# Chunk rounds of a hybrid mixer: queries turned and squared by ScalarE, solved blocks stored twice, row minima in nine visits

## The chip, the cores and the metric

One core of a Trainium2 chip runs the whole kernel in one launch. The metric is the device time of an execution in microseconds (us), and the median over several runs counts. Engines are named as in the profile: PE (TensorE matmuls), PEld (its weight loads), DVE (VectorE), ACT (ScalarE), POOL (GpSimd) and SP (SyncE, which issues the DMAs here). Each engine works through its own list in order and waits on semaphores.

## The reference

One layer on x (1024 tokens, width 1024), all in float32:

```
h    = rms_norm(x);  proj = h @ w_in
gdn  : q,k,v = silu(causal_conv(proj)); l2-normalised q,k; 4 heads of 128
       per chunk: A = strictly lower (beta k k^T * decay)
                  w = solve(I + A, beta k exp(g)); u = solve(I + A, beta v)
       v_new = u - w S;  o = (q exp(g)) S + (q k^T * decay) v_new;  S = S exp(g_last) + k_dec^T v_new
       o = rms_norm(o) * silu(gate)
pool : trailing-window means minus the token, a 64x64 map per group
mla  : 4 heads, q,k of 96, v of 64; softmax over all keys of chunks up to the query's own
x    = x + concat(gdn, pool, mla) @ w_out
x    = x + (silu(h2 @ w_gate) * (h2 @ w_up)) @ w_down,   h2 = rms_norm(x)
```

## The kernel before

The kernel runs in stages. The input projection makes tiles of 128 columns for all tokens. The chunk rounds do the delta rule and the attention together. The output projection and the feed-forward network follow, where PE works on matmuls of 512 columns almost without a pause.

**The rounds.** A chunk has 128 tokens here (eight chunks, i = 0 to 3 and b = 0 or 1, chunk 2i + b), all four heads at once. Chunk b has two PSUM banks, `U[b]` and `W[b]`. The stages of one chunk, by their names in the orders: `pre` (ACT squares q, from `qkvf` into `kd`), `qk` (PE: k times q into W; then the sums of q's squares by eight one-column instructions, L2322, into U), `turn` (PE transposes k and v), `m0` (PE turns the solved diagonal blocks `N0` by multiplying with the identity, L2334; ACT copies them to `M0`, a view of `M_`, L1379), `x1`, `y1`, `m1`, `x2`, `y2` (the inverse is put together from blocks: products on PE, copies on ACT, differences on DVE), `ks` (k and q times the state S), `tr` (the inverse applied), `av` (attention in the chunk and the new state), `oms`, `on` and `ot` (norm and turn of the output). The 32x32 diagonal blocks of all chunks are solved beforehand by DVE (`base_inverses`, 31 steps, L1804 and L1807), written to DRAM (`inverse_kept`, L783) and read back chunk by chunk as `N0` (L811 and L795).

**The attention.** For a head, the score products `st:g.kt` (L2393) go to banks 5 and 6, ACT takes the exponential (L1402), and `pv:g.kt` (L2405) multiplies by the values into bank 7. The exponential needs a bound for each query: the minimum of negated scores. `mx:t.part` (L2237) computes the scores of query tile t with the queries along the partitions into bank 4, and DVE reduces them (L1787). Twelve such visits make a head. `mr` then multiplies the minima, broadcast along one side, with the identity (L2245, two visits of four matmuls), so that they stand as a row, and ACT copies the row into row 96 of the queries (`low_row`, L1327). Head i + 1 has its maxima in round i; head 0 has them between the matmuls of the last projections (`FIRST_MAXIMA`), on banks 4 and 5 in turn.

**The order.** `PE_ORDER`, `ACT_ORDER`, `DVE_ORDER` and `POOL_ORDER` are written out by hand, stage by stage, as `stage:which:round`. SP goes through `PE_ORDER` too and issues a chunk's next loads at `ks`, `tr` and `av`, and the loads of a head at `st:0.3`. After the orders the stages of the last chunk (`AFTER_ROUNDS`) are spread over the output projection's first matmuls (L2432).

Of the kernel before, what the change touches and what calls it, by code (L numbers as in the profile page):

```python
# [13 lines left out]
P = 128  # L14
# [47 lines left out]
def hybrid_block(nc, logs_d, e_d, a_d, diag_d, n_d, qkv_d, q_d, k_d, mask_d, x2_d, hid_d, hs_d, wt_d, x, positions, attn_norm, w_in, conv_w, a_log, dt_bias, gdn_out_norm, pool_w, pool_scale,  # L62
# [27 lines left out]
    ident_r = Region(c.at).take("ident_r", [P, P], f32r)  # L90
# [17 lines left out]
    q_low = c.take("q_low", [P, TT], f32r)  # L108
# [59 lines left out]
    n_base = r.take("n_base", [P, BASE, BASE])  # L168
    solve_tmp = Region(R3_REST + 8 * 1024).take("solve_tmp", [P, BASE * BASE // 4])
# [74 lines left out]
    assert r.at <= R1 + 104 * KB  # L244
    A_, B_ = [A0, A1], [B0, Region(R1 + 110 * KB).take("B1", [P, 4, P])]
# [36 lines left out]
    with ctx:  # L282
# [83 lines left out]
        logs_kept, kk_done = sem("log_sums_kept"), sem("kk_done")  # L366
# [20 lines left out]

        def maxima(h):
            tiles = [("mx", (t, part), h) for g in GROUPS for t in range(4 * g + 3, 4 * g - 1, -1) for part in range(g + 1)]
            return tiles + [("mr", g, h) for g in GROUPS]  # L390

        LOW_TILES = [w for st, w, _ in maxima(0) if st == "mx"]

        def low_bank(w, h):
            return 4 if h else 4 + LOW_TILES.index(w) % 2

        UNITS = [(g, kt) for g in GROUPS for kt in range(4 * g + 4)]
        mp = Steps(sem("att_max_pe"), [f"mx{w[0]}.{w[1]}" if st == "mx" else f"mr{w}" for st, w, _ in maxima(0)])
        md = Steps(sem("att_max_dve"), [n for g in GROUPS for n in
                                        [f"low{t}.{part}" for t in range(4 * g + 3, 4 * g - 1, -1) for part in range(g + 1)] +  # L400
                                        (["lows"] if g else [])])
        ma = Steps(sem("att_max_act"), [f"row{g}" for g in GROUPS])
# [15 lines left out]
        def entries(text):  # L418
# [8 lines left out]
            st:1.0:0 st:1.1:0 mx:7.0:1 pv:1.0:0 mx:7.1:1 pv:1.1:0 st:1.2:0 mx:6.0:1 st:1.3:0 st:1.4:0 st:1.5:0  # L427
            mx:6.1:1 pv:1.2:0 mx:5.0:1 st:1.6:0 pv:1.3:0 mx:5.1:1 pv:1.4:0 mx:4.0:1 qk:0:0 qk:1:0 st:1.7:0 turn:0:0
            turn:1:0 st:0.0:0 pv:1.5:0 mx:4.1:1 pv:1.6:0 m0:0:0 m0:1:0 x1:0:0 mx:3.0:1 st:0.1:0 x1:1:0 mx:2.0:1
            pv:1.7:0 st:0.2:0 st:0.3:0 mx:1.0:1 y1:0:0 pv:0.0:0 pv:0.1:0 mx:0.0:1 m1:0:0 mr:1:1 x2:0:0 y1:1:0 mr:0:1  # L430
            y2:0:0 st:1.0:1 ks:0:0 pv:0.2:0 mx:7.0:2 m1:1:0 tr:0:0 x2:1:0 pv:0.3:0 mx:7.1:2 av:0:0 mx:6.0:2 pv:1.0:1
            y2:1:0 st:1.1:1 st:1.2:1 mx:6.1:2 ks:1:0 st:1.3:1 mx:5.0:2 st:1.4:1 st:1.5:1 ot:0:0 mx:5.1:2 tr:1:0
            qk:0:1 mx:4.0:2 turn:0:1 av:1:0 mx:4.1:2 m0:0:1 pv:1.1:1 pv:1.2:1 x1:0:1 pv:1.3:1 y1:0:1 mx:3.0:2
            pv:1.4:1 st:1.6:1 m1:0:1 st:1.7:1 pv:1.5:1 x2:0:1 ot:1:0 st:0.0:1 y2:0:1 qk:1:1 ks:0:1 turn:1:1 st:0.1:1
            tr:0:1 mx:2.0:2 m0:1:1 st:0.2:1 pv:1.6:1 st:0.3:1 mx:1.0:2 x1:1:1 pv:1.7:1 mx:0.0:2 av:0:1 y1:1:1
            pv:0.0:1 mr:1:2 pv:0.1:1 pv:0.2:1 m1:1:1 pv:0.3:1 st:1.0:2 x2:1:1 mr:0:2 st:1.1:2 y2:1:1 mx:7.0:3 ot:0:1
# [201 lines left out]
        def _(sp):  # L638
# [87 lines left out]
            for m in range(1, IN_ALL + KEEP_LAG):  # L726
# [1844 lines left out]
```

## Time and profile before

| | |
|---|---|
| median of 3 runs | 1221.44 us (1221.03 to 1224.62) |
| profiled execution | 1224.1 us, span 1222.3 us |
| PE busy | 1203.0 us, 98% |
| DVE, ACT, POOL busy | 809.7, 447.0, 397.6 us |
| chunk rounds | 307.9 to about 476.5 us of the span |

A row of the timeline gives the start, the time from the first instruction's start to the last one's end, the engine, the line and the number of merged instructions. Matmuls overlap, so the time that one takes from PE is read from one start to the next. A float32 matmul is two instructions, a transpose one. "Idle before" with a releaser in brackets is a wait.

### The profile page before, as it was taken

How to read it: one execution, taken by the hardware profiler on the slowest of the kernel's cores; microseconds unless marked ns; L12 is line 12 of the kernel's file. 1: busy time of each engine (PE TensorE's matmuls, PEld its weight loads, DVE VectorE, ACT ScalarE, POOL GpSimd, SP SyncE). 2: the span in 40 equal slices, each digit the busy share in tenths (PEclk: the TensorE clock that was granted, in tenths of full speed). 3: DMA queues.
4: the chain of work that ended last, by engine and by line, in shares of the span. 5: the costliest groups of instructions: out<-in, count | busy, mean ns of one | idle time of the engine just before them, and what ended most of it. 6: DMA issues, size and time to landing. Idle time of an engine off the chain costs nothing.

```text
span 1222.3 us, 16782 instructions
## 1 busy us (share of the span) xinstructions
PE 1203.0 (98%) x6225; PEld 989.2 (81%) x6225; DVE 809.7 (66%) x1235; ACT 447.0 (37%) x730; POOL 397.6 (33%) x363
## 2 busy tenths in 40 slices
PE   8999999999999999999999999999999999999998
PEld 7887777887788888888788888888888887888877
DVE  6537777898567764445756656565565688777686
ACT  6322322442334232244533333333333353435242
POOL 6001111540112221015736656675565446000000
PEclk9999999999999999999999999999999999999999
DMA  8311344672842310324147465644674369565544
GB/s 251 96 36 35 104 128 123 194 230 79 259 121 75 92 53 1 121 103 128 46 138 232 164 207 181 215 171 139 223 289 151 100 211 308 165 199 168 173 127 169
DMA packets 191779, 183.54 MB, mean 150 GB/s; under 512 B 19853, under 2 KB 148227, under 8 KB 191698
## 3 DMA queue, kind: packets, MB, share of 16 engines
q1 hardware_dynamic: 191574, 182.43, 47.2%
q8 instruction: 50, 0.82, 0.3%
q14 instruction: 31, 0.25, 0.1%
q10 hardware_dynamic: 124, 0.04, 0.0%
HBM read 125.70 MB, written 55.68 MB: 148 GB/s over the span
## 4 chain that ended last, share of the span: by engine, by line
PE 90%; DVE 5%; ACT 1%; issue 1%; POOL 1%; DMA 1%; DVEq 0%; POOLq 0%; ACTq 0%
PE ps L2522 33%; PE ps L2126 18%; PE ps L2527 14%; PE ps L2432 5%; PE ps L2295 3%; PE ps L2393 3%; PE ps L2405 3%; PE ps L2102 1%; DVE wop_lo L1989 1%; DVE xop L1973 1%; PE ps L2300 1%; PE ps L2237 1%; PE ps L2197 1%; PE ps L2093 1%; DMA wd_raw<-in_w_down 1%
## 5 line engine op out<-in xcount | busy, mean ns | idle before, releaser
L2522 PE MATMUL ps<-xop,wop_hi 128*128 128x512 f32 x1232 | 381.4, 391 | 1.7 <-DVE wop_lo L1989 1.0
L2522 PEld LDWEIGHTS ps<-xop,wop_hi 128*128 128x128 f32 x1232 | 230.7, 188 | 52.8 <-DVE wop_lo L1989 2.3
L2522 PE MATMUL ps<-xop,wop_lo 128*128 128x512 f32 x616 | 240.4, 390 | 0.0
L2527 PE MATMUL ps<-dop,wop_hi 128*128 128x512 f32 x440 | 136.9, 392 | 3.6 <-DVE x L2071 3.4
L2522 PEld LDWEIGHTS ps<-xop,wop_lo 128*128 128x128 f32 x616 | 115.6, 188 | 24.9
L1989 DVE TENSOR_TENSOR wop_lo<-w_sumS,wop_hi 128x512 fp32r<-128x512 f32 (+1 forms) x104 | 85.7, 827 | 69.2 <-ACT wop_hi L1462 69.2
L1989 DVE TENSOR_TENSOR wop_lo<-w_pair,wop_hi 128x512 fp32r<-128x512 f32 (+1 forms) x76 | 86.1, 1134 | 37.2 <-ACT wop_hi L1462 37.2
L2126 PE MATMUL ps<-act_hi,w_hi 128*128 128x512 f32 x320 | 104.0, 406 | 0.0
L2071 DVE TENSOR_TENSOR x<-x,ps 128x512 f32<-128x512 f32 x112 | 76.6, 684 | 39.2 <-PE ps L2527 39.0
L2527 PEld LDWEIGHTS ps<-dop,wop_hi 128*128 128x128 f32 x440 | 81.9, 188 | 24.2 <-DVE wop_lo L1989 4.2
L2126 PE MATMUL ps<-act_lo,w_hi 128*128 128x512 f32 x320 | 98.7, 390 | 0.0
L2126 PE MATMUL ps<-act_hi,w_lo 128*128 128x512 f32 x320 | 98.6, 389 | 0.0
L2527 PE MATMUL ps<-dop,wop_lo 128*128 128x512 f32 x220 | 86.0, 391 | 0.0
L1462 ACT ACTIVATE wop_hi<-w_sumS 128x512 fp32r<-128x512 f32 (+1 forms) x104 | 63.2, 609 | 58.5 <-PE ps L2522 42.8
L2126 PEld LDWEIGHTS ps<-act_hi,w_hi 128*128 128x128 f32 x320 | 58.7, 188 | 14.7 <-issue 2.6
L2126 PEld LDWEIGHTS ps<-act_lo,w_hi 128*128 128x128 f32 x320 | 60.1, 188 | 12.8
L2126 PEld LDWEIGHTS ps<-act_hi,w_lo 128*128 128x128 f32 x320 | 60.1, 188 | 12.7
L1462 ACT ACTIVATE wop_hi<-w_pair 128x512 fp32r<-128x512 f32 (+1 forms) x76 | 46.4, 611 | 60.2 <-PE ps L2522 47.8
L1582 DVE TENSOR_TENSOR w_lo<-raw,w_hi 128x1024 fp32r<-128x1024 f32 x20 | 25.6, 1281 | 53.2 <-ACT w_hi L1263 53.1
L1167 POOL TENSOR_TENSOR w_sumS<-w_pair 128x512 f32<-128x512 f32 (+1 forms) x26 | 33.8, 1300 | 67.4 <-DVE wop_lo L1989 53.2
L2527 PEld LDWEIGHTS ps<-dop,wop_lo 128*128 128x128 f32 x220 | 41.3, 188 | 9.0
L1704 DVE SCALAR_TENSOR_TENSOR stage<-ps,cols,stage 128x1023 f32<-128x1023 f32 (+2 forms) x36 | 46.0, 1279 | 0.7
(338 smaller groups left out, 2166.1 us busy)
## 6 DMA issues: line engine op xcount, KB each, us to landing
w_pair<-in_w_gate_up SPq DMA_DIRECT2D x44, 512.0 KB, 5.2
hidden<-up SPq DMA_DIRECT2D x22, 512.0 KB, 3.0
wd_rows<-in_w_down SPq DMA_DIRECT2D x22, 512.0 KB, 5.2
raw<-in_w_in SPq DMA_DIRECT2D x21, 512.0 KB, 4.5
wd_raw<-down_sums SPq DMA_DIRECT2D x12, 768.0 KB, 8.3
down_sums<-wd_rows SPq DMA_DIRECT2D x33, 256.0 KB, 2.6
wd_raw<-in_w_down SPq DMA_DIRECT2D x9, 768.0 KB, 8.0
qkv_kept<-qkv_st SPq DMA_DIRECT2D x12, 512.0 KB, 5.3
```

Source lines behind the costliest of these rows:

```text
L1167: pool.tensor_tensor(s1, a21, a22, ALU.add).then_inc(sums_ready, 1)
L1462: act.activation(wop_hi[q % RING][:, 0:kh, :], src, ACT.Copy).then_inc(wop_high, 1)
L1704: op = dve.scalar_tensor_tensor(dst[:, d:SEQ], src[:, 0:SEQ - d], tap(3 - d), dst[:, d:SEQ], ALU.mult, ALU.add)
L1989: dve.tensor_tensor(wop_lo[q % RING][:, 0:kh, :], src, wop_hi[q % RING][:, 0:kh, :].bitcast(f32), ALU.subtract).then_inc(wop_ready, 1)
L2071: dve.tensor_tensor(part, part, bank, ALU.add).then_inc(added, 1)
L2126: last = pe.matmul(ps[0:rows, pair + h, :], w[:, k, 0:rows], a[:, k, h * BANK:(h + 1) * BANK], start=(k == 0 and w is whi and a is a_hi), ...
L2295: last = pe.matmul(ps[:, out_bank, h * P:(h + 1) * P], lhs(h), rhs(h), start=True, stop=True)
L2393: pe.matmul(ps[:, 5 + UNITS.index(b) % 2, 0:n], keys_h[i % 2][0:KROWS, kt * P:(kt + 1) * P].bitcast(f32), qrys_h[i % 2][0:KROWS, first:fir ...
L2405: last = pe.matmul(ps[:, 7, at:at + V_DIM + 1], expT[UNITS.index(b) % 4][:, (t - first) * P:(t - first + 1) * P], V[:, kt, i, :], start=(k ...
L2432: last = pe.matmul(ps[:, op_pair[t] + h, :], o, w[:, k, h * BANK:(h + 1) * BANK], start=(k == 0 and len(parts) == 2 and w is w_out_hi), st ...
L2522: last = pe.matmul(ps[:, bank, :].rearrange("p (t n) -> p t n", n=P), w[:, k, :], a[:, k, :, :], start=(p in ("P1", "P2", "P7") and k == 0 ...
L2527: last = pe.matmul(ps[:, bank, :], w[:, k, :], a[:, k, :], start=(p in ("P1", "P2", "P7") and k == 0 and w is wop_hi[s] and a is hi), stop ...
```

## The change

- **q's squares.** Behind `qk`, PE transposes q of the four heads into bank U (step `qT`) in place of the one-column sums. ACT squares each head's 128x128 out of PSUM with a sum over its row into `tok_sc` columns 44 to 47, and DVE takes the sums from there. ACT's `pre` waits for `qT` now.
- **Solved blocks.** POOL writes a transposed copy of all solved blocks (`n_turned`), SP scatters it to a second DRAM tensor `nt_d` beside `n_d` (which is cleared beforehand as `n_d` is) and loads it chunk by chunk straight into `M0`. The stage `m0` goes from PE and ACT (POOL's product of that name stays).
- **Row minima.** The twelve tiles of a head are packed into nine bank visits. After the last one PE transposes the minima once; ACT copies 8 rows of 128 negated to `low_rows`, and SP moves them by a DMA (`turn_rows`) into the queries' row. The score products of that head, and the first minima visit for the head after it, wait for that DMA (`rows_turned`).
- **Orders.** All four orders are written anew. Of the head's minima in the projection, the places are four in one tile and six in the next.

```diff
+        LOW_TILES = [((7, 0),), ((7, 1),), ((6, 0),), ((6, 1), (4, 1)), ((5, 0),), ((5, 1), (1, 0)), ((4, 0),), ((3, 0),), ((2, 0), (0, 0))]
...
         PE_ORDER = entries("""
+            mx:0:1 st:1.0:0 st:1.1:0 mx:1:1 pv:1.0:0 st:1.2:0 st:1.3:0 mx:2:1 pv:1.1:0 pv:1.2:0 mx:3:1 st:1.4:0
+            st:1.5:0 mx:4:1 st:1.6:0 qk:0:0 mx:5:1 qk:1:0 st:1.7:0 turn:0:0 pv:1.3:0 pv:1.4:0 mx:6:1 st:0.0:0 st:0.1:0
+            turn:1:0 pv:1.5:0 pv:1.6:0 mx:7:1 pv:1.7:0 x1:0:0 x1:1:0 y1:0:0 mx:8:1 st:0.2:0 y1:1:0 m1:0:0 pv:0.0:0
+            st:0.3:0 m1:1:0 x2:0:0 mr:0:1 x2:1:0 y2:0:0 pv:0.1:0 ks:0:0 pv:0.2:0 pv:0.3:0 mx:0:2 tr:0:0 y2:1:0 mx:1:2
...
+            st:0.2:1 mx:8:2 y2:0:1 x2:1:1 pv:1.6:1 st:0.3:1 pv:1.7:1 mr:0:2 ks:0:1 pv:0.0:1 tr:0:1 pv:0.1:1 y2:1:1
+            mx:0:3 av:0:1 mx:1:3 st:1.0:2 ks:1:1 mx:2:3 pv:0.2:1 pv:0.3:1 tr:1:1 st:1.1:2 st:1.2:2 av:1:1 st:1.3:2
...
+            mr:0:3 y2:1:2 st:0.3:2 pv:0.0:2 ks:1:2 st:1.0:3 pv:0.1:2 tr:1:2 st:1.1:3 ot:0:2 av:1:2 st:1.2:3 pv:0.2:2
+            pv:0.3:2 qk:0:3 pv:1.0:3 pv:1.1:3 turn:0:3 pv:1.2:3 st:1.3:3 x1:0:3 ot:1:2 st:1.4:3 y1:0:3 qk:1:3 pv:1.3:3
+            m1:0:3 turn:1:3 x2:0:3 pv:1.4:3 y2:0:3 x1:1:3 st:1.5:3 ks:0:3 y1:1:3 st:1.6:3 tr:0:3 st:1.7:3 st:0.0:3
+            av:0:3 pv:1.5:3 pv:1.6:3 pv:1.7:3 st:0.1:3 st:0.2:3 pv:0.0:3 st:0.3:3 m1:1:3 pv:0.1:3 pv:0.2:3 pv:0.3:3
+            x2:1:3 ot:0:3 y2:1:3
...
 SP
+            def turn_rows(h):
+                sp.wait_ge(ma.sem, ma.after("rows", h))
+                sp.dma_start(qrys_h[h % 2][QK:QK + 1, :].bitcast(f32),
+                             low_rows[h % 2][0:TT, :]).then_inc(rows_turned, 16)
+            keep_solved(n_d, n_base)
+            def load_turned(b, c):
+                sp.dma_start(M_[b][:, 0:2, :].rearrange("p a n -> p (a n)"),
+                             nt_d[:, c, :, :].rearrange("p h n -> p (h n)")).then_inc(n_loaded[b], 16)
+            sp.wait_ge(filled, 5)
+            keep_solved(nt_d, n_turned)
-            sp.wait_ge(n_kept, 16 * P // BASE)
+            sp.wait_ge(n_kept, 2 * 16 * P // BASE)
 POOL
+            pool.wait_ge(n_solved, 1)
+            pool.tensor_copy(n_turned[:, :, :], n_base[:, :, :].rearrange("p i j -> p j i")).then_inc(filled, 1)
 ACT
+            def low_row(h):
+                act.wait_ge(mp.sem, mp.after("mr0", h))
+                act.activation(low_rows[h % 2][0:TT, :], ps[0:TT, 4, 0:P], ACT.Copy, scale=-1.0).then_inc(ma.sem, 1)
...
-                        gsig(b, act.activation(kd[b][:, :, :], qkvf[b][:, 0:4, :], ACT.Square))
+                        gafter(gp[b], "qT")
+                        for h in range(4):
+                            op = act.activation(kd[b][:, h, :], ps[:, U[b], h * P:(h + 1) * P], ACT.Square,
+                                                accum_out=tok_sc[b][:, 44 + h:45 + h])
+                        gsig(b, op)
 DVE
-                        gafter(gp[b], "norms")
+                        gafter(ga[b], "sq")
-                        gsig(dve.tensor_scalar(sc[:, 0:4], ps[:, U[b], 0:4], EPS, None, ALU.add))
+                        gsig(dve.tensor_scalar(sc[:, 0:4], sc[:, 44:48], EPS, None, ALU.add))
 PE
-                    for j in range(4):
-                        last = pe.matmul(ps[:, 4, j * P:(j + 1) * P], q_low[:, 4 * w + j:4 * w + j + 1].broadcast_to([P, P]),
-                                         ident_r[:, :], start=True, stop=True)
+                    last = pe.transpose(ps[:, 4, 0:P], q_low[:, :], ident[:, :])
...
-                        for h in range(4):
-                            last = pe.matmul(ps[:, U[b], h:h + 1], kd[b][:, h, :], ones[:, 0:1], start=True, stop=True)
+                        four_t(U[b], q, cnt)
...
-                    elif stage_name == "m0":
-                        pe.wait_ge(n_loaded[b], i * 16 + 16)
...
-                        gafter(ga[b], "m0")
+                        pe.wait_ge(n_loaded[b], 2 * (i * 16 + 16))
```

## Rows read from the trace of the kernel before

**Rows 1.** The page, part 1: busy time of each engine.

```profile
PE 1203.0 (98%) x6225; PEld 989.2 (81%) x6225; DVE 809.7 (66%) x1235; ACT 447.0 (37%) x730; POOL 397.6 (33%) x363
```

**Rows 2.** Stretches: busy PE, PEld, DVE, ACT, POOL; granted PE clock, DMA share, GB/s.

```profile
307.00:476.50 169.50, 166.97 (x1509) 140.40 (x1508) 113.23 (x249) 57.01 (x121) 35.52 (x30) 0.99 0.36 108
...
345.00:385.00 40.00, 40.00 (x361) 34.50 (x360) 29.90 (x64) 14.65 (x32) 9.52 (x8) 1.00 0.37 108
...
425.00:476.50 51.50, 50.24 (x458) 42.51 (x458) 31.29 (x71) 16.72 (x37) 10.51 (x9) 1.00 0.12 34
```

**Rows 3.** Waits of PE in the rounds: total, times, longest.

```profile
PE ps L2295 <- DVE N L1887: 1.3, 1, 1.3
PE ps L2405 <- ACT expT L1402: 1.1, 1, 1.1
```

**Rows 4.** PE's timeline in the rounds.

```profile
330.07 1.15 PE L2334 MATMUL ps<-ident,N 64*64 64x64 f32 x32
...
443.60 0.68 PE L2334 MATMUL ps<-ident,N 64*64 64x64 f32 x16
444.21 0.66 PE L2245 MATMUL ps<-ident_r,q_low 128*128 128x128 f32 x4
444.71 1.93 PE L2393 MATMUL ps<-qh,kh 105*128 105x512 f32 x4
...
447.19 2.00 PE L2405 MATMUL ps<-V,expT 128*128 128x65 f32 x16
449.02 0.60 PE L2300 MATMUL ps<-ident,N 128*128 128x128 f32 x4
449.56 0.68 PE L2350 MATMUL ps<-N,qkvf 64*64 64x64 f32 x16
...
451.81 0.95 PE L2322 MATMUL ps<-ones,kd 128*128 128x1 f32 x8
452.69 0.41 PE L2356 MATMUL ps<-ident,N 64*64 64x64 f32 x4
```

**Rows 5.** Groups of PE by line: count | busy us, mean ns | idle before.

```profile
L2322 PE MATMUL ps<-ones,kd 128*128 128x1 f32 x64 | 7.6, 240 | 0.0
...
L2334 PE MATMUL ps<-ident,N 64*64 64x64 f32 x128 | 5.2, 223 | 0.0
```

**Rows 6.** Groups of ACT by line and form.

```profile
L1376 ACT ACTIVATE kd<-qkvf 128x512 f32<-128x512 f32 x8 | 5.0, 622 | 0.6 <-DMA qkvf<-qkv_kept 0.5
...
L1327 ACT ACTIVATE qh<-ps 1x512 fp32r<-1x512 f32 x8 | 4.7, 590 | 12.0 <-PE ps L2245 11.8
...
L1402 ACT ACTIVATE expT<-ps 128x128 f32<-128x128 f32 x8 | 2.2, 274 | 6.5 <-PE ps L2393 6.4
...
L1242 ACT ACTIVATION_READ_ACCUMULATOR prep<-raw 128x1 f32 x4 | 0.7, 186 | 0.0
```

**Rows 7.** DMA issues: size, median us to landing.

```profile
inverse_kept<-n_base SPq DMA_DIRECT2D x4, 128.0 KB, 3.2
...
inverse_kept<-n_base SPq DMA_DIRECT2D x1, 128.0 KB, 2.3
```

**Rows 8.** DVE's timeline, from head 0's minima to the rounds.

```profile
284.53 0.62 DVE L1787 TENSOR_REDUCE q_low<-ps 128x1 fp32r<-128x256 f32 x2 [0.54 <-PE ps L2237]
...
309.23 0.19 DVE L1807 TENSOR_TENSOR n_base<-n_base,solve_tmp 128x31 f32<-128x31 f32 x1
...
310.13 0.69 DVE L1787 TENSOR_REDUCE part_low<-ps 128x1 f32<-128x512 f32 x1 [0.17 <-PE ps L2237]
```

**Rows 9.** One stretch at half the clock; columns as in rows 2.

```profile
314.00:315.00 1.00, 1.00 (x3) 0.45 (x2) 0.00 (x0) 0.00 (x0) 0.00 (x0) 0.50 0.79 160
```

**Rows 10.** SP's timeline: DMA issues in the rounds.

```profile
309.45 2.57 SPq L783 DMA_DIRECT2D inverse_kept<-n_base  x4
...
318.47 3.83 SPq L811 DMA_DIRECT2D N<-inverse_kept  x2
322.35 4.45 SPq L814 DMA_DIRECT2D w_out_sb<-in_w_out  x8
...
382.08 0.23 SPq L685 DMA_DIRECT2D qh<-mask_rows  x1
...
385.13 0.40 SPq L801 DMA_DIRECT2D A<-keys_kept  x1
```

More of the change, by code:

```diff
@@ L107, in hybrid_block @@
     part_low = c.take("part_low", [P, 2, 4])
-    q_low = c.take("q_low", [P, TT], f32r)
+    q_low = c.take("q_low", [P, P])
     o_scale = c.take("o_scale", [P, 4])
@@ L244, in hybrid_block @@
     assert r.at <= R1 + 104 * KB
+    low_rows = [Region(R1 + 96 * KB + 512 + 512 * b).take(f"low_rows{b}", [P, P]) for b in range(2)]
     A_, B_ = [A0, A1], [B0, Region(R1 + 110 * KB).take("B1", [P, 4, P])]
@@ L386, in hybrid_block, with low_cols, low_bank @@
         GROUPS = (1, 0)
-        def maxima(h):
[L389 to L395, printed above, removed]
-        UNITS = [(g, kt) for g in GROUPS for kt in range(4 * g + 4)]
[L398 to L402, printed above, removed]
+        LOW_TILES = [((7, 0),), ((7, 1),), ((6, 0),), ((6, 1), (4, 1)), ((5, 0),), ((5, 1), (1, 0)), ((4, 0),), ((3, 0),), ((2, 0), (0, 0))]
+        LAST_LATE = max(at for at, tiles in enumerate(LOW_TILES) if any(t >= 4 for t, part in tiles))
+        def low_cols(at):
+            out, first = [], 0
+            for t, part in LOW_TILES[at]:
+                n = min(BANK, (t + 1) * P - part * BANK)
+                out.append((t, part, first, n))
+                first += n
+            assert first <= BANK
+            return out
+        def maxima(h):
+            tiles = [("mx", at, h) for at in range(len(LOW_TILES))]
+            return tiles + [("mr", 0, h)]
+        def low_bank(at, h):
+            return 4 if h else 4 + at % 2
+        UNITS = [(g, kt) for g in GROUPS for kt in range(4 * g + 4)]
+        mp = Steps(sem("att_max_pe"), [f"{st}{w}" for st, w, _ in maxima(0)])
+        md = Steps(sem("att_max_dve"), [n for at in range(len(LOW_TILES)) for n in [f"low{at}"] + (["lows"] if at == LAST_LATE else [])])
+        ma = Steps(sem("att_max_act"), ["rows"])
+        rows_turned = sem("att_max_rows_turned")
         tp = Steps(sem("att_scores"), [f"s{g}.{kt}" for g, kt in UNITS])
@@ L432, in hybrid_block @@
[L432 to L436, printed above, removed]
@@ L798, in load_chunk @@
                     sp.dma_start(E_[b][:, :, :], e_d[c, :, :, :]).then_inc(e_loaded[b], 16)
+                elif part == "ot":
+                    sp.wait_ge(gd[b].sem, gd[b].after("on", i - 1))
+                    load_turned(b, c)
                 else:
@@ L2272, in _ @@
                 if m == M_GATE + 2:
-                    pe.wait_ge(ma.sem, ma.after(f"row{GROUPS[1]}", 0))
+                    pe.wait_ge(ma.sem, ma.after("rows", 0))
                     pe.wait_ge(a_ready, TT)
```

175 lines of the change are left out of this document (76 added, 99 removed).

## The prediction

> **What bounds the kernel now.** The page comes first: PE is busy 98% of the span at the full clock, DVE 66%, ACT 37% [rows 1]. So time leaves this kernel where PE has less to do or less to wait for. The stretches say where the change acts: the chunk rounds run from 307.9 us, where the last projection ends, to 476.5 us. There PE is busy 166.97 of 169.50 us, DVE 113, ACT 57, and from 345 to 385 us PE has no gap [rows 2]. Two waits stand in the rounds, 1.3 us at their end and 1.1 us at their start [rows 3]. Nearly every microsecond of PE work taken out of the rounds is therefore a microsecond of the kernel, provided that the new orders leave no new gap and the new transfers land in time. The rest (the projection before, the output projection and the feed-forward behind) is PE work back to back and only shifts.
>
> **Part 1: the solved blocks stored turned (stage m0 gone).** PE spends 443.60 to 444.21 = 0.61 us on the 16 instructions of one m0 [rows 4]; there are 128 of them in all [rows 5], eight stages: 8 x 0.61 = **-4.9 us**. An ACT copy of 0.38 us goes too, off the path. Neither comes back on PE; the turned blocks come by DMA.
>
> **Part 2: q's squares.** The eight column sums of a chunk (L2322) take 451.81 to 452.69 = 0.88 us [rows 4], and back to back some less (64 of them are 7.6 us busy, overlapping [rows 5]); I take 0.84. In their place PE turns q: four transposes, 449.02 to 449.56 = 0.54 us [rows 4], less where they follow their own kind; I take 0.49. 8 x (0.84 - 0.49) = **-2.8 us**. ACT squares four times 128x128 out of PSUM instead of once 128x512 (0.62 us). No row has that form; a 128x128 exponential from PSUM takes 0.27 us, and the squares of x with a sum (L1242) each have a read of the sum behind them, 0.19 us [rows 6]. So four cost 4 x 0.46 = 1.8 us, or 1.5 where they overlap by 0.1 as successive ones do, on an engine one third busy. But they are now in a chain: q turned, squares, DVE's sum (0.16), then PE may write v's transposes over the bank: with handovers of 0.1, 1.9 to 2.2 us. DVE waits there too, with its bank minima queued behind, and ACT waits for PE in the middle of the exponentials. In the new PE order I added up what stands between q's transposes and v's (k's own four transposes, 0.44, are always among it): least is chunk 1 of the last round, a pv of four blocks, an m1 and k's, 0.9 + 0.34 + 0.44 = 1.7 us (two such pv are 447.19 to 449.02 [rows 4]); two others have 2.1 and 2.2, the rest more. So **+0.6 us** (0.4 there, 0.2 at the two), bounds 0 and 2; without this cover it would be 8 x 2.
>
> **Part 3: row minima.** The matmuls (12 a head) and DVE's reductions stay, with nine bank visits for twelve. A lone 512-column visit costs about 0.1 us more than a projection matmul's 0.23, but each tile still loads its own weights; I take 0, bounds 0 to -0.9. The broadcast of minima to a row goes: 2 x 0.50 us a head (444.21 to 444.71) against one transpose of about 0.15. In three rounds 3 x 0.85 = **-2.6 us**. Head 0's lies in the projection and would give 0.65 more, but see part 4. The row itself now goes PSUM, ACT (0.3), SP issue (0.25 to 0.35), DMA: the shortest landing in the rows is 2.3 us for 128 KB [rows 7], so about 3.4 us with handovers, where ACT's 0.59 us copy had been enough [rows 6].
>
> **Part 4: the start of the rounds.** Head 0's visits end with three reductions behind two adjacent visits, where before two small ones did (284.53 to 285.07) [rows 8]: 0.69 + 0.56 + 0.28 less overlap ends about 0.75 us later. DVE's solver runs without a pause from there to 309.4, then clears S and does the first reduction to 310.8. In the new order PE has only one minima visit and two score products (2.2 us) before the second visit, which needs that reduction: now about 311.6. Before, PE waited until 311.10 for ACT, with one visit fewer done. Head 0's 0.65 us is lost in a longer wait, and **+0.5 us** comes on top. Behind this wait the clock was half (granted 0.50 at 314 us) [rows 9], about 3.7 us of half speed; the wait gets longer, so I keep it: 0, from -1.8 (the stretch goes) to +1.8 (twice as long).
>
> **Part 5: transfers.** SP's queue at the start: the solved blocks' scatter, chunk loads, pool rows, N0, w_out [rows 10]. The change adds a second scatter (same 4096 pieces of 128 bytes; 3.2 us to landing when alone [rows 7]), two loads of 128 KB, and SP waits for the scatter before N0 and w_out. SP's issues stand one behind the other from 309.45 to 326.8 us, and what is issued lands later than it did alone, so all behind moves by some 3.5 + 0.7 us. By my sum: second scatter issued 316.3 to 319, landed near 325.7; N0 and turned blocks issued to 327.7, landed about 330. PE reaches the first x1 (m0's 330.07 [rows 4], plus a score product and a visit more, less two q sums, plus the late start) at 331.3. It holds, with about 1 us. w_out lands near 340.5, needed by ACT's first split at 338 to 340: nobody is behind it in a hurry. Head 2's rows follow in the queue, land 342.5 to 343; row 1's DMA is behind them on SP, and mx:0:2 waits for both. PE comes there 11.3 us after the first x1, at 342.6. In round 1 the same: after st:0.3:1 SP issues head 3 (3.0 us from 382.08 to the next kind at 385.13 [rows 10]), then row 2, landed 5.7 us after; PE has 5.2 us of work. In the last round mr:0:3 to st:1.0:3 is y2 0.6, st 0.27, pv 0.9, ks 1.8 = 3.6 us against 3.4. Sum **+1.5 us**, bounds 0 and 5. The four zero stores (1 MB) more near 41 us, POOL's copy of the turned blocks (1024 columns; a clear of 1024 takes 0.96 us, a 128x512 product 1.3, so 1 to 3 us, needed only at 315.5) and the later load of turned blocks into M (after "on", 7 us ahead of use) cost 0: PE there has four raw tiles ahead.
>
> **Part 6: orders, and the end.** I laid each dependence of the new PE order (x1 to y1, y1 to m1, m1 to x2, ks to tr, tr to av, av to the next ks) against the work that stands between, an ACT copy at 0.4 us, a DVE operation at 0.7, a handover at 0.1: all covered, the tightest by 0.1 to 0.2 us, so 0; bounds 0 to +4. The last y2 has only the turn of o in front and nothing between it and ks:1:3; DVE's oT (0.75 us) and y2 (0.41) set ks: idle about 0.9 instead of 1.3 [rows 3]: **-0.4 us**. What is behind it stays.
>
> Sum: -4.9 - 2.8 + 0.6 - 2.6 + 0.5 + 1.5 - 0.4 = **-8.1 us**. The profiled execution took 1224.1 us with a span of 1222.3; its like after would be 1216.0 with a span of 1214.2. The runs' median is 1221.44, 2.7 below it, and the difference is carried over: **1213.3 us**.
>
> **A rule against it.** The row goes by DMA now: 4 KB three times in the rounds. In the rows a transfer of 128 KB lands in 2.3 us at best [rows 7], and the work that stands before its reader is 3.6, 5.2 and over 7 us, so it is priced only where that is short. The Trainium skill, "DMA: Bandwidth & Descriptors" (Rules for kernel authors), warns that under 64 KB a transfer is mostly overhead, and ("Anatomy of one DMA") puts that at about 2.0 us. By that rule, with nothing in front, the change would lose 3 x 2.0 us more, a sum of -2.1; by the rows the wait is covered but for what part 5 counts. Rival (b) is this case, priced from the rows.
>
> **Rivals.**
> (a) Nothing of part 5 is late and the half-speed stretch shortens or the visits save: 1213.3 - 1.5 - 2 = 1209.8. For it: the transfers are covered on average. Chance 0.2.
> (b) The row's DMA and the head loads are late in each round, 2 to 3 us at three places, and N0 too: 1213.3 + 5 = about 1218. For it: SP issues without a pause to 326.8 us, and the margins are about 1 us; against: the queue is nearly empty afterwards (34 GB/s from 425 us on [rows 2]). Chance 0.14.
> (c) Slower: ACT's squares wait for PE in the middle of the exponentials. If q's turn, the squares and DVE's sum aren't covered, each of 8 chunks pays 1.5 us, and the exponential queued behind holds pv as long again: 8 x 1.5 = 12 us and more, 1221 to 1227. It takes the gain from 8.1 / 8 = 1.0 us uncovered a chunk and is slower by more than 0.3% from (8.1 + 3.7) / 8 = 1.5; I count 0.4 at the worst. Chance 0.06.
> (d) The rounds become bound by their chain (ks, r, tr, v, av, S) and not by PE: a chunk's chain is about 7 us and PE's work per chunk is 169/8 = 21 us, so no; at most a few gaps: 1217. Chance 0.06.
> The forecast itself, 1211 to 1216: 0.54.
>
> A difference of 0.3% is 3.7 us. Faster by more (below 1217.8): the forecast, (a), most of (d), half of (b): 0.86. Within: the rest of (b) and a part of (c): 0.09. Slower: 0.05. The range leaves out the ends of (a), (b) and all of (c): 1209.5 to 1218.
>
> **What would show it.** m0 and the column sums gone from PE's lines and 32 more transposes under 0.14 us apart; the stretch from the last projection matmul to the output projection 7 to 9 us shorter; first wait of the rounds over 2 us, ended by DVE's reduction; waits on DMA at mx:0:2 and mx:0:3 under 1.5 us. It would be wrong if PE's waits in the rounds add up to more than 8 us, or if the clock falls a second time.

## The result, and the profile after

The changed kernel takes **1211.38 us** (median of 6 runs, 1209.13 to 1212.1) against 1221.24 us of the kernel before (6 runs, 1219.62 to 1224.62): ratio 0.991, 95% interval 0.9897 to 0.9923. The forecast was 1213.3 us in a range of 1209.5 to 1218.0. Its profiled execution took 1210.15 us with a span of 1208.4.

The page, part 1, of the kernel after (of before: [rows 1]):

```profile
PE 1185.0 (98%) x6037; PEld 978.5 (81%) x6037; DVE 809.1 (67%) x1235; ACT 445.6 (37%) x774; POOL 398.4 (33%) x364
```

188 matmuls are gone: 128 of m0, 64 column sums and 32 broadcasts, against 32 transposes of q and 4 of the minima. PE's busy time fell by 18 us, the span by 13.9. The stretches of the kernel after, with the columns of [rows 2]: the rounds, two middle parts, and one stretch behind the longest wait.

```profile
306.00:471.50 165.50, 156.42 (x1342) 132.29 (x1340) 115.69 (x254) 58.82 (x171) 37.78 (x32) 0.97 0.41 120
...
345.00:385.00 40.00, 39.79 (x354) 34.08 (x352) 32.32 (x68) 14.38 (x43) 9.29 (x9) 1.00 0.35 101
425.00:466.00 41.00, 41.00 (x368) 34.96 (x367) 29.88 (x65) 14.09 (x43) 10.50 (x9) 1.00 0.20 58
...
332.00:338.00 6.00, 6.00 (x47) 5.79 (x49) 3.60 (x9) 0.69 (x2) 3.43 (x3) 0.50 1.01 404
```

From 345 us on PE is full, as before. The loss sits ahead of that: of 165.5 us of rounds PE is idle for 9, and the granted clock, 0.99 before, is 0.97. The waits of PE in the rounds (of before: [rows 3]):

```profile
PE ps L2324 <- DVE attn L1893: 4.6, 1, 4.6
PE ps L2265 <- DVE part_low L1814: 2.1, 1, 2.1
PE ps L2445 <- issue: 1.0, 1, 1.0
PE ps L2265 <- DMA qh<-low_rows: 0.7, 2, 0.5
PE ps L2319 <- DVE N L1916: 0.7, 1, 0.7
```

The second is the wait at the start that part 4 foresaw. The first I had named nowhere. PE's timeline shows where it is (turn:1:0, where k and v of chunk 1 are transposed in the first round), DVE's what holds it, and SP's why. PE's:

```profile
310.31 0.50 PE L2265 MATMUL ps<-kh,qh 105*128 105x512 f32 x1 [2.10 <-DVE part_low L1814]
...
331.86 1.97 PE L2324 MATMUL ps<-ident,qkvf 128*128 128x128 f32 x8 [4.63 <-DVE attn L1893]
```

DVE's, which starts again when the pool rows have landed:

```profile
329.08 0.55 DVE L1866 MEMSET N<- 64x256 f32 x2 [6.00 <-DMA oT<-pz]
329.64 0.69 DVE L1901 TENSOR_TENSOR kd<-ps,decays 128x512 f32<-128x512 f32 x1
```

SP's, the order in which the transfers were issued:

```profile
309.01 2.70 SPq L796 DMA_DIRECT2D inverse_kept<-n_base  x4
...
317.51 4.73 SPq L796 DMA_DIRECT2D inverse_turned_kept<-n_turned  x4
322.29 1.76 SPq L832 DMA_DIRECT2D oT<-pz  x2
325.48 0.34 SPq L835 DMA_DIRECT2D N<-inverse_kept  x1
...
328.10 5.09 SPq L839 DMA_DIRECT2D w_out_sb<-in_w_out  x8
...
344.44 0.73 SPq L787 DMA_DIRECT2D qh<-low_rows  x1
```

DVE clears corners of N where the pool rows lay (`clear_corners`), so it waits until `oT<-pz` has landed. The second scatter stands ahead of these rows on SP's queue, and the new DVE order has this step (turn:0:0) ahead of qk:1:0. So chunk 1's `attn`, for which nothing was missing, comes late, and PE with it.

The clock record of the trace has two half-speed stretches in the rounds: 3.4 us from 311.3, behind the start's wait, and 6.8 us from 331.8, at the end of the wait of 4.6 us. Before there was one of 3.4 us [rows 9].

**Where the time went.** From the first minima visit or score product to the first output product the rounds take 471.46 - 306.10 = 165.4 us, before 479.62 - 307.91 = 171.7: -6.3. Ahead of them it is -1.8, behind them 742.7 - 736.9 = -5.8. The sum is the 13.9 of the two profiled spans. In the medians it is 9.9, because the profiled execution of before lay 2.9 above the median of six and that of after 1.2 below.

### The profile page after: what moved, and what is told of

Its sections match the earlier page's. It is cut to its first block, busy times and chain, and to the rows that moved or that the text cites. A ratio compares the mean times of both kernels' runs of the same rounds, so it can differ in the third digit from the quotient of the medians.

```text
span 1208.4 us, 16451 instructions
## 1 busy us (share of the span) xinstructions
PE 1185.0 (98%) x6037; PEld 978.5 (81%) x6037; DVE 809.1 (67%) x1235; ACT 445.6 (37%) x774; POOL 398.4 (33%) x364
## 4 chain that ended last, share of the span: by engine, by line
PE 86%; DVE 7%; issue 2%; SPq 1%; POOL 1%; ACT 1%; DMA 1%; DVEq 0%; POOLq 0%; ACTq 0%
PE ps L2535 32%; PE ps L2155 17%; PE ps L2540 15%; PE ps L2445 5%; PE ps L2319 3%; PE ps L2418 2%; PE ps L2406 2%; DVE wop_lo L2018 1%; PE ps L2131 1%; PE ps L2324 1%; DVE xop L2002 1%; DVE solve_tmp L1833 1%; DVE n_base L1836 1%; PE ps L2226 1%; PE ps L2122 1%
## 5 line engine op out<-in xcount | busy, mean ns | idle before, releaser
L1186 POOL TENSOR_TENSOR w_sumS<-w_pair,w_sumS 128x512 f32<-128x512 f32 (+1 forms) x26 | 35.5, 1364 | 34.5 <-DVE wop_lo L2018 34.5
```

Source lines behind the costliest of these rows:

```text
L1186: pool.tensor_tensor(w_sum["S4"][:, 0:kh, :], w_pair[n % 2][0][:, kh:2 * kh, :], w_sum["S2"][:, 0:kh, :], ALU.subtract).then_inc(sums_read ...
```

## The experiments

Each was timed beside the kernel before, whose median lay between 1221.5 and 1222.2 us; the ratio is to it, with its 95% interval in brackets. "after" is the changed kernel, 1211.38 us with a ratio of 0.991 (0.9897 to 0.9923). Times of two kernels are called different here where these intervals don't overlap.

**The pool rows first (e1).** Theory A: the second scatter delays the pool rows, and its wait is all that is lost.

```diff
-            keep_solved(nt_d, n_turned)
             for p in range(2):
                 sp.dma_start(oT[:, :, 4 + p, :], pz[:, p, :]...).then_inc(pool_moved, 16)
+            keep_solved(nt_d, n_turned)
```

> Changed kernel with one swap on SP: the two pool-row transfers (oT<-pz) are issued ahead of the second scatter instead of behind it. Theory A (the 4.6 us wait at turn:1:0 is DVE held in clear_corners by pool_moved, late because the second scatter stands in front of the pool rows): DVE's clear_corners runs about 2 to 3 us earlier, the 4.6 us wait falls under 2 us and the 6.8 us stretch at half the clock behind it goes; 1211.4 - 3 - 3.4 = about 1205, range 1203 to 1208. Rival B (the queue as a whole is late: without that wait PE only waits as long for the solved blocks at the first x1, since N0 and the turned blocks land later by what the scatter takes): 1211 to 1212, with a wait of 3 to 4 us at x1 by a DMA. Rival C (ACT's squares hold DVE): no change of the wait at all.

1216.24 us, ratio 0.9952 (0.9937 to 0.9966): 5 us slower than after. Theory A falls, and so does the number of rival B (1211 to 1212). The profiled execution took 2418 us, with PE's matmuls at about twice their usual length, so its rows can't be compared; e4 below has the same queue and a usable trace.

**DVE's order (e2).** qk:1:0 ahead of turn:0:0 on DVE, the queue as in after.

> Changed kernel with one swap in DVE's order of round 0: qk:1:0 before turn:0:0, as the kernel before had it; transfers as in the changed kernel. Theory A with the order as its second half: the pool rows land as late as in the changed kernel, but only turn:0:0 stands behind them, PE gets past turn:1:0 without the wait and then waits at x1 for DVE's kd, Vn of both chunks: about 1 to 2 us of the 4.6 come back and the half-speed stretch may stay: 1208 to 1211. If only the order was at fault: the wait goes as in the other kernel, 1204 to 1206. If neither matters: 1211.4.

1212.68 us, 0.9928 (0.991 to 0.9945): not different from after. The wait at turn:1:0 is gone. Two others came in its place, 4.1 us for the row's DMA at mx:0:2 and 2.1 us at 331.6 us for DVE, which now sits behind the pool rows one step later (the other 2.1 us of the second line are the start's, as in after):

```profile
PE ps L2265 <- DMA qh<-low_rows: 4.5, 2, 4.1
PE ps L2265 <- DVE part_low L1814: 4.2, 2, 2.1
```

**No second scatter (e3).** e1 with `keep_solved(nt_d, ...)` left out: the turned blocks read as zero, so the delta rule's output isn't computed, but every instruction of the engines stays.

> As the kernel with the pool rows first, but the second scatter isn't issued at all and SP waits for the first alone (the turned blocks in DRAM then hold zeros; the output of the delta rule is not the reference's). Price of the second scatter where it stands once the pool rows are ahead of it. Theory A: 0 to -1 us against the kernel with the pool rows first (N0 and w_out are 4 us earlier and nothing waited for them). Rival B: 3 us and more faster than it.

1208.81 us, 0.989 (0.9872 to 0.9908). Against e1, which differs by the scatter alone, that is 7.4 us, as e3's rival B had it; the 2.6 us against after are within the intervals. The only wait over 1 us is the start's 2.1, but behind it the clock was half for 13.7 us.

**A product of V ahead of the second visit (e4).** e1, and pv:1.0:0 ahead of mx:1:1 in PE's order.

> The kernel with the pool rows first, and in PE's order of round 0 the first value product pv:1.0:0 ahead of the second minima visit mx:1:1, which waits for DVE's first reduction behind the solver. My account of the start (that wait, 2.1 us, is DVE's and lies beside work that PE could do): pv:1.0 runs in it, its exponential being ready near 309.4, so 0.7 to 0.9 us less than the kernel with the pool rows first. If the wait is ACT's as before the change: no difference.

1215.5 us, 0.9946 (0.9931 to 0.9961). That is 0.7 us below e1, as expected in size but within the intervals. The start's wait fell to 1.2 us (for ACT), and no half-speed stretch stood there. But PE came earlier to the next readers:

```profile
PE ps L2265 <- DMA qh<-low_rows: 7.7, 1, 7.7
PE ps L2324 <- DVE attn L1893: 2.9, 1, 2.9
```

In e2 and e4 the wait moved on and didn't go. The transfers between 309 and 343 us are late as a whole, and whichever reader PE reaches first waits. The trace of e4 also shows how e1's queue is later than after's: with the pool rows ahead of it the second scatter's last part was issued at 325.7 us and not at 321.7, the first load of N at 328.9 and not at 325.5, the last load of w_out landed at 347.8 and not at 343.0, and the wait at mx:0:2 ended at 350.9 us and not at 347.9.

**Loads early (f1), and pv first besides (f2).** Chunk 1's q, k, v, the E and A of both chunks and the pool rows issued ahead of the wait for the solved blocks (both), and pv:1.0:0 ahead of mx:1:1 (the second).

```diff
             turn_rows(0)
+            sp.wait_ge(gemm_done, IN_ALL)
+            sp.wait_ge(mid_act.sem, mid_act.after("pool1"))
+            # qkvf[1], E and A of both chunks, pool rows
             sp.wait_ge(n_solved, 1)
```

> Changed kernel, with SP's loads that don't need the solved blocks (second chunk's rows, E, A, and the pool rows: 2.8 MB) issued when the last projection is done, ahead of the wait for the solver, instead of behind the first scatter. Theory B as it stands now (the DMA queue of the start of the rounds is the bound: swapping two transfers in it only moved the wait, without the second scatter it was gone): everything in the queue is 3 to 6 us earlier, the pool rows land before 318 us, the solved blocks before 326, w_out by 336; the 4.6 us wait at turn:1:0 and the wait for the row's DMA go, and the long half-speed stretch behind the 4.6 us goes too: 1211.4 - 4.6 - 2 = about 1205, range 1202 to 1208. Rival D (what holds PE is not the queue but DVE's order): wait at turn:1:0 stays, 1210 to 1212.

> The same with pv:1.0:0 ahead of the second minima visit in PE's order. The start's own wait falls from 2.1 to about 1.2 us (so much was seen with it in the run before), and, if the half-speed stretch at 311 us hangs on that wait's length, it goes too: 0.8 us, and up to 1.7 more, below the kernel with early loads alone. If PE's clock goes its own way, only 0.8.

1213.96 us (0.993, 0.9916 to 0.9944) and 1212.61 us (0.9921, 0.9908 to 0.9935): no better than after, and the 1205 us of the theory did not come. The longest wait of f1, and of f2:

```profile
PE ps L2265 <- DMA qh<-low_rows: 6.9, 2, 6.5
```

```profile
PE ps L2265 <- DMA qh<-queries_kept: 5.0, 1, 5.0
```

The pool rows are in time now: no wait is left at turn:1:0, and 1.2 (f1) and 1.4 us (f2) are left at x1 for the turned blocks. Late is mx:0:2, whose loads stand behind the eight of w_out, 4 MB issued from 328 us, of which ACT in after splits the first at 344.6 us and the last at 457. SP's timeline of f1, and PE's:

```profile
328.56 4.36 SPq L839 DMA_DIRECT2D w_out_sb<-in_w_out  x8
...
337.47 0.73 SPq L787 DMA_DIRECT2D qh<-low_rows  x1
```

```profile
347.20 0.77 PE L2265 MATMUL ps<-kh,qh 105*128 105x512 f32 x1 [6.49 <-DMA qh<-low_rows]
```

The row of 4 KB was issued at 337.5 us and PE could go on at 347.2; w_out's last load had landed at 344.1.

**w_out out of the way (g2, g3).** Two of the eight loads stay in place; six go behind the row DMA of head 2. g2 is f2 with this, g3 is e2 with it.

```diff
-            for half in range(2):
-                for k in range(half * 4, half * 4 + 4):
-                    sp.dma_start(w_out_sb[:, k, :], ...).then_inc(w_out_loaded, 16)
+            for k in range(2):
+                sp.dma_start(w_out_sb[:, k, :], ...).then_inc(w_out_loaded, 16)
...
                     turn_rows(i)
+                    if i == 1:
+                        sp.wait_ge(w_out_loaded, 2 * 16)
+                        # the same for k in range(2, TT)
...
-                        act.wait_ge(w_out_loaded, TT * 16)
+                        act.wait_ge(w_out_loaded, (2 if k < 2 else TT) * 16)
```

> The chunks' loads and the pool rows early, pv:1.0:0 ahead of mx:1:1 (f2_loads_early_pv), and of w_out's eight loads only two ahead of the rounds' loop; the other six are issued behind the row DMA of head 2. Theory of the queue (rival B in another place): in f2_loads_early_pv TensorE waited 5.0 us at mx:0:2 for head 2's transfers, which stood behind 4 MB of w_out. If so, this wait falls below 1 us, the half-speed stretch behind it goes with it, and the time is 5 to 8 us below f2's 1212.6: 1205 to 1208 us. Rival, the queue is full whatever stands in it and in which order: the wait moves on to the loads of the next chunks behind w_out (mx:1:2, qk:0:1, pre:0:1) and the time stays at 1211 to 1214 us.

> The kernel after with qk:1:0 ahead of turn:0:0 on VectorE (e2_dve_order) and w_out's last six loads behind the row DMA of head 2. e2 had no wait at turn:1:0 but 4.1 us at mx:0:2 for the row DMA. Theory of the queue: this wait falls below 1 us and the time is 4 to 6 us below e2's 1212.7: 1206 to 1209 us. Rival: scatter 2 and the first M and N loads are what is late, so TensorE waits at x1 or x2 instead, and the time stays at 1210 to 1213 us.

1205.3 us (0.9867, 0.9846 to 0.9888) and 1207.2 us (0.9881, 0.9864 to 0.9897): 7.3 and 5.5 us below the same kernels with w_out in the way, as the theory of the queue had it. The wait at mx:0:2 for head 2's loads and row is gone in both; the 0.7 us for a row's DMA that each has left stands at mx:0:3. (The six loads moved leave the place in front of the row and also the time in which it moves; which of the two counts, the order on the queue or the shared bandwidth, no run tells apart.) g3 still waits 4.0 us, until 332.7 us, for DVE, which sits behind the pool rows. g2 waits at x1: the profile puts it down to "issue", but SP issued the turned blocks' first load at 327.07 us and it landed 2.5 us later, at 329.6. Behind this wait its clock was half. PE's timeline and a stretch of g2:

```profile
329.68 0.68 PE L2359 MATMUL ps<-M,B 64*64 64x64 f32 x16 [1.70 <-issue]
```

```profile
330.00:346.00 16.00, 15.62 (x127) 13.60 (x123) 3.54 (x8) 3.60 (x10) 0.00 (x0) 0.51 0.51 168
```

This profiled execution of g2 took 1212.56 us at a clock of 0.992; three others of the same kernel had 0.999 and took 1204.0 to 1205.3, one had 0.993 and took 1210.2.

**x1 covered (g4).** g2, and mx:8:1 and st:0.2:0 ahead of x1:0:0 in PE's order, pv:0.0:0 ahead of y1:1:0.

> g2_early_and_late with mx:8:1, st:0.2:0 and pv:0.0:0 moved ahead of or in among x1:0:0 to y1:1:0 in TensorE's order. In g2 TensorE waited 1.7 and 0.4 us at x1 (the turned blocks' load), and behind this wait a half-speed stretch of 17 us lay in the profiled execution (clock 0.992, 1212.6 us), while three other executions of it had a clock of 0.999 and took 1204.0 to 1205.3 us. Theory, the half-speed stretches start only behind a wait of TensorE, and cost half their length: with the last larger wait covered the stretch does not come, every run is at 1202 to 1205 us and none at 1210 to 1213. Rival, the clock falls by chance, also without such a wait: the same spread of 1204 to 1213 us as g2. Rival, the moved stages open new waits on DVE or ACT in the chain x1 to m1: 1206 to 1210 us.

**1203.44 us** (6 runs, 1201.68 to 1210.72), 0.986 (0.9839 to 0.9882): the lowest median of all, 7.9 us below after; the 1.9 us to g2 are within the intervals. Its waits:

```profile
PE ps L2421 <- ACT expT L1432: 1.2, 1, 1.2
PE ps L2448 <- issue: 1.0, 1, 1.0
PE ps L2268 <- DVE q_low L1817: 0.8, 1, 0.8
PE ps L2322 <- DVE N L1919: 0.7, 1, 0.7
PE ps L2268 <- DMA qh<-low_rows: 0.6, 1, 0.6
```

Five runs had a clock of 0.999 or 1.000 and took 1201.7 to 1203.9 us; one had 0.993 and took 1210.72. So the first theory's "none at 1210" is refuted: the clock can still fall with x1 covered, in one of six executions here and in two of five in g2, too few to say that it falls more rarely. The execution in which it fell has no trace.

**The control.** The kernel before, its last six loads of w_out moved in the same way.

> The control: the kernel before with w_out's last six loads behind head 2's, as in g2, g3 and g4. Theory, the late queue is a product of the change (second scatter, turned loads, row DMA), and the kernel before waited for no DMA in the rounds: 1220.5 to 1222 us, no difference. Rival, w_out's 4 MB slow down also the old kernel's start by contention or by what ends its 1.1 us wait: 1215 to 1219 us.

1221.91 us (11 runs), ratio 1.000 (0.9992 to 1.0009). The old kernel had nothing to gain there; the late queue came with the change.

**Part 2 undone, part 1's products put back**, each in the kernel after. In the first, ACT also squares q as it lies and DVE reads the sums from PSUM again, as before the change; in the second nobody reads what the products write. PE's side of the two:

```diff
-                        four_t(U[b], q, cnt)
+                        for h in range(4):
+                            last = pe.matmul(ps[:, U[b], h:h + 1], kd[b][:, h, :], ones[:, 0:1], start=True, stop=True)
```

```diff
                     elif stage_name == "x1":
+                        for h in range(4):
+                            for rows_p in PAIR:
+                                pe.matmul(corner(W[b], rows_p, h), N0[b][rows_p, h, :], ident[rows_p, rows_p], start=True, stop=True)
```

> The kernel after with part 2 undone: ScalarE squares q as it lies, TensorE sums the four columns with products of one column each, no q turned for it. My sum had 2.8 us for this part as a gain on TensorE and 0.6 as a loss on ScalarE's chain, so 2.2 us slower than after: 1213 to 1214.5 us. Rival, the part is worth nothing because the 32 one-column products ran beside others: 1210.5 to 1212 us. Rival, one-column products cost more than their records show, as they end a run of one kind: over 1215 us.

> The kernel after with the eight m0 products of each chunk put back on TensorE into the bank that the old kernel used, ahead of x1; nobody waits for them, the turned blocks still come from DRAM, and the output is the reference's. My sum had 4.9 us for 64 of them: 1215.5 to 1217 us. Rival, TensorE waits at x1 for the turned blocks anyway, or has slack in the rounds: 1211 to 1213 us.

1216.85 us (0.9959, 0.9944 to 0.9974) and 1216.99 us (0.9953, 0.9936 to 0.997). Undoing part 2 costs 5.5 us where 2.2 was expected, and falls, as a number, into that run's last rival; putting m0 back costs 5.6 us, where 4.9 was the term. Neither time is the price of the instructions alone. A group and waits of PE with part 2 undone:

```profile
L2344 PE MATMUL ps<-ones,kd 128*128 128x1 f32 x64 | 8.0, 245 | 1.0 <-ACT kd L1404 0.9
```

```profile
PE ps L2263 <- DMA qh<-queries_kept: 2.0, 2, 1.4
...
PE ps L2344 <- ACT kd L1404: 0.9, 2, 0.6
```

The column sums in this order wait for ACT's squares, 0.6 us of it at 440 us with a half-speed stretch of 3.4 us starting 2.6 us behind it, and in all this execution has 13.6 us at half speed in the rounds where after has 10.2. Counted from start to start as in the table below, its rounds are 4.7 us longer than those of after: 3.3 us of sums against transposes at the full clock (2.8 was the term), 1.2 of other work, 1.7 of half speed, and 1.5 less of waits. With m0 back the rounds are 6.8 us longer: 3.8 us of m0's products at the full clock, 2.0 of waits (5.4 us at turn:1:0), 1.2 of half speed and 0.2 less of other work. So each part's price is confirmed to within about a microsecond, and the rest of each difference comes from waits, the clock and what lies outside the rounds.

## Why the prediction was right, and where it wasn't

The time, the sign and the likeliest case held. But two signs that I had named for a wrong prediction came true as well (waits of PE over 8 us: 9.1; a second fall of the clock), and the rounds became 6.3 us shorter, not 7 to 9. Inside the sum, errors of 4 to 7 us lie against each other, so that the total came within 2 us of the forecast is in good part luck. To see them, each group of PE's timeline in the rounds was given the time from its start to the next group's start, less the waits in brackets. "g4" stands beside before, chosen because the clock was full in all its rounds.

| PE's work in the rounds, us | before | g4 | difference | my term |
|---|---|---|---|---|
| 64x64 products with the identity (m0 and others) | 7.74 | 2.70 | -5.0 | -4.9 |
| column sums, and 128x128 transposes of q and k | 13.63 | 10.78 | -2.9 | -2.8 |
| minima to a row | 3.11 | 0.59 | -2.5 | -2.6 |
| minima visits | 13.02 | 9.76 | -3.3 | 0 |
| products of V and score products | 65.17 | 64.04 | -1.1 | 0 |
| everything else | 65.5 | 63.9 | -1.6 | 0 |
| all | 168.2 | 151.8 | -16.4 | -10.3 |

Of the 16.4, 1.7 is the half-speed stretch of before, which lay over visits (0.6) and score products (1.1). The work itself fell by 14.7 us, 4.4 more than my terms. The same sum for after is 156.3 with 10.2 us of half speed in it, so 151.2 of work: 15.3 less than before (166.5).

**Parts 1, 2 and 3's broadcast: right, to 0.1 us each.** Reading them from one start to the next priced them. The runs that undo them agree to about a microsecond (3.8 us of m0's products, 3.3 of column sums).

**Part 3, the visits: the term was mis-sized.** I took 0 with a bound of -0.9 for nine visits in place of twelve; in the three heads of the rounds, 27 visits in place of 36, it is -3.3 us in the table and -2.7 without the half speed of before. The rows that I should have read start to next start were there. PE's timeline of before, a lone tile of 384 and one of 128 columns with the work behind them:

```profile
408.17 0.44 PE L2237 MATMUL ps<-kh,qh 105*128 105x384 f32 x1
408.45 1.00 PE L2405 MATMUL ps<-V,expT 128*128 128x65 f32 x8
...
420.72 0.31 PE L2237 MATMUL ps<-kh,qh 105*128 105x128 f32 x1
420.95 0.68 PE L2343 MATMUL ps<-M,B 64*64 64x64 f32 x16
```

And PE's timeline of g4, a pair of tiles in one visit, and a lone tile of 512:

```profile
358.10 0.48 PE L2268 MATMUL ps<-kh,qh 105*128 105x256 f32 x2
358.42 1.24 PE L2409 MATMUL ps<-qh,kh 105*128 105x384 f32 x4
...
361.63 0.48 PE L2268 MATMUL ps<-kh,qh 105*128 105x512 f32 x1
361.95 0.38 PE L2409 MATMUL ps<-qh,kh 105*128 105x128 f32 x2
```

The lone 128-column tile shown holds PE for 0.23 us and the lone 384 for 0.28 (over the six of each in the rounds of before 0.14 to 0.24 and 0.28 to 0.67); both tiles of a pair together take 0.32, as one of 512 alone. The groups say the same in means: tiles of 384, 256 and 128 columns 569, 370 and 306 ns before, 442, 322 and 221 after.

**Part 2's chain: covered.** ACT's squares and reads start 0.25 us apart, not the 0.38 to 0.46 that I took. ACT's timeline in after, the first of four heads, and DVE's sum:

```profile
321.08 0.28 ACT L1404 ACTIVATE kd<-ps 128x128 f32<-128x128 f32 x1 [1.64 <-PE ps L2324]
321.25 0.19 ACT L1404 ACTIVATION_READ_ACCUMULATOR kd<-ps 128x1 f32 x1
321.35 0.27 ACT L1404 ACTIVATE kd<-ps 128x128 f32<-128x128 f32 x1
```

```profile
322.25 0.17 DVE L1896 TENSOR_SCALAR tok_sc<-tok_sc 128x4 f32<-128x4 f32 x1 [0.92 <-ACT kd L1404]
```

q's transposes ended at 321.04 us (320.44 and 0.60) and DVE's sum at 322.42, so the chain is 1.4 us where I had 1.9 to 2.2. No wait of PE hangs on it in after: +0.6 should have been 0, and rival (c) did not occur.

**Part 4: the wait of 2.1 us by DVE's reduction came as written**, at 310.3 us, 1.3 us earlier than I put it, mostly because the kernel is a microsecond ahead there, with a half-speed stretch of 3.4 us as before (I had read that one as 3.7).

**Part 5: the step that failed.** I summed "+1.5 us, bounds 0 and 5" from margins at x1, mx:0:2 and mx:0:3, and PE waited there for 0.7 us in all. But the margins held only because PE was late itself: I had head 2's loads and the row landed at 342.5 to 343 us and PE there at 342.6, and in after the loads let PE go on at 347.9, w_out's last one having landed at 343.0 and not at 340.5. I had the pool rows in SP's queue, but left out that DVE waits for them: 4.6 us at turn:1:0 and 3.4 us for the half-speed stretch behind it, 8.0 together. I had written that the new orders were covered, bounds 0 to +4, by laying PE's dependences against PE's work; of DVE's waits on transfers I checked none. The experiments show that this wait isn't the cause but the place: removed or shortened, it came back as 4.1 to 7.7 us at mx:0:2 (what rival (b) had for three places, in e2, f1, f2 and e4). Only with w_out's six loads moved behind them, or without the second scatter (e3), did that go. My remark that "nobody is behind it in a hurry", it being w_out, was the wrong reading: head 2's loads and the row DMA stood behind it.

**The rule on small transfers.** The Trainium skill, "DMA: Bandwidth & Descriptors" (Rules for kernel authors), calls a transfer under 64 KB mostly overhead, and its section "Anatomy of one DMA" puts the fixed part at about 2.0 us, for transfers that GpSimd issues; these are issued from SP. By that figure 3 x 2.0 us would have come on top, an estimate. No run here shows a 4 KB transfer by itself. The row's DMA cost 0.7 us of waits in after and 0.6 in g4, so here it is covered, as the rows said, and the 3 x 2.0 us did not come; where it was late (4.1 to 7.7 us), head 2's loads and the row stood behind 4 MB.

**Part 6, the end:** the wait for N fell from 1.3 to 0.7 us, and a third wait of before that I had not listed, 1.16 us for B ahead of the first output product, became 1.0 of "issue": -0.8 for -0.4.

The balance of the rounds: work -15.3, waits 9.1 for 3.6 = +5.5, half speed +3.4 (10.2 us for 3.4, at half their length): -6.4, measured -6.3. (It closes by construction, since work is what the waits and the half speed leave.) I had -10.3 and +2.2. The rest of the median's 9.9, 3.6 us, lies outside the rounds, which I had at nothing (below).

What stays open: how much of e1's 5 us is the later queue that e4 shows, why the unchanged part behind the rounds became quicker, and how long a half-speed stretch gets. Behind the start's wait of 2.1 us it was absent (f1, g3, m0 put back), 3.4 us (after, e2), 10.2 us (part 2 undone) or 13.7 us (e3).

## What to carry to other kernels

When a change adds transfers to a full queue, list every reader behind them on every engine, also those of a later stage, and move the bulk load that is needed last (here 3 MB of weights) out of the way before reordering compute; removing one wait at a time only shows the next reader. Price a lone small matmul between others by its start to the next start, and count what two of them in one visit would take. A wait of PE costs its length and can cost a stretch of half clock behind it, which stood behind 13 of the 17 waits of over 1.5 us in the traces here. And where a total comes out right, lay the measured terms beside your own before you believe the sum.

## What was not expected of the hardware

**The clock splits the runs of one kernel.** In g4 a mean granted clock of 0.993 against 0.999 to 1.000 goes with 1210.7 against 1201.7 to 1203.9 us. An estimate from the clock fits: a mean of 0.993 over 1209 us is 2 x 0.007 x 1209 = 17 us at half speed, which costs 8.5 us if half of that time is lost; measured 7.5. In all profiled executions with a trace, each half-speed stretch within the rounds begins during or up to 3 us behind a wait of PE of 0.6 us or more. The reverse doesn't hold: 13 of the 17 waits over 1.5 us had one, and 6 of the 29 between 0.6 and 1.5. That the wait brings it on is argued from this order in time and not shown by a run. All six runs of after lay at 0.994 to 0.996, so it paid this every time. Of 52 runs of the kernel before beside the experiments, five lay at 0.996 and took 1224.9 to 1225.9 us; the others lay at 0.998 to 1.000.

**The feed-forward became quicker, though nothing in it was changed.** In equal stretches of 200 us, at the full clock and with the same waits, PE did 871 matmuls after for 867 before, and 884 for 879. Before, and after:

```profile
579.60:779.60 200.00, 197.43 (x867) 161.21 (x866) 123.97 (x137) 78.65 (x136) 120.83 (x85) 1.00 0.52 169
779.60:979.60 200.00, 200.00 (x879) 164.65 (x878) 116.26 (x126) 72.30 (x126) 114.67 (x79) 1.00 0.53 179
```

```profile
571.40:771.40 200.00, 197.41 (x871) 162.18 (x870) 124.37 (x137) 78.61 (x136) 120.64 (x86) 1.00 0.52 171
771.40:971.40 200.00, 200.00 (x884) 165.59 (x883) 115.45 (x125) 73.51 (x128) 113.98 (x78) 1.00 0.53 178
```

The part behind the rounds takes 737.0 us in g4 and 736.9 in after, but 742.7 in before and 741.1 in the control. All kernels with the change show it (736.9 to 739.6). The matmuls behind the rounds are the same 3248 in each. Read from one start to the next and less the waits of over 0.15 us, they take 729.7 us in before, 729.9 in the control, and 725.1 in both after and g4. Most of them take 227 ns, but 490 of before and 487 of the control take 232 to 245 ns, against 53 of after and 58 of g4. So of the 5.8 us between before and after here some 4.6 are this and 1.1 are waits (6.0 against 4.8 us). That is a third of the 13.9 us between the two profiled executions, and close to half of the medians' 9.9 if it is the same in every execution, and it comes from code that the change doesn't touch. No experiment was made on the cause.
